# The last feed-forward output blocks computed by token halves, with the final norm of one half between the matmuls of the other

## The reference, cut to what matters

```python
def rmsnorm(x, g):
    y = x * lax.rsqrt(jnp.mean(x * x, axis=-1, keepdims=True) + EPS)
    return y * g
...
for l in range(DEPTH):                       # DEPTH = 1
    ...                                      # attention, gated DeltaNet, merge: x += gt1 * (...)
    h = rmsnorm(x, norm2_g[l]) * (1.0 + sc2) + sh2
    gate, up = jnp.split(h @ w_ffn_in[l], 2, axis=-1)
    x = x + gt2 * ((jax.nn.silu(gate) * up) @ w_ffn_out[l])
return rmsnorm(x, final_g)
```

## Time and profile before

| what | value |
|---|---|
| time, median of 3 runs | 1871.59 us (1869.07 to 1871.85) |
| the profiled execution, own time | 1867.37 us |
| its span in the trace | 1865.7 us |
| PE busy | 1775.3 us, 95% |
| DVE busy | 892.4 us, 48% |
| ACT busy | 473.4 us, 25% |
| mean granted clock of TensorE | 0.972 |

### The profile page before, as it was taken

The page is one execution under the profiler, slowest core; times in us unless marked ns, Lnnn a source line. Parts: engine busy times, 40 slices in busy tenths (PEclk is TensorE's granted clock), DMA queues, the critical chain, the costliest instruction groups (busy, mean ns, idle before and its releaser), DMA issues.

```text
span 1865.7 us, 22580 instructions
## 1 busy us (share of the span) xinstructions
PE 1775.3 (95%) x8387; PEld 1424.8 (76%) x8387; DVE 892.4 (48%) x1231; ACT 473.4 (25%) x861; POOL 164.4 (9%) x208
## 2 busy tenths in 40 slices
PE   5998879999999999999899979999999999999997
PEld 5876768888767777677678868888888888888876
DVE  6675566667534444444554344243333324333336
ACT  3334422222243333343321222111111111111101
POOL 1125551111001001010000000000000000000000
PEclk7899999999999999999999979999999999999998
DMA  7745555666423231340445110222022012102002
GB/s 246 213 117 171 173 167 181 180 183 187 130 76 108 74 82 65 91 129 34 163 165 192 54 53 26 65 68 57 12 67 66 29 40 67 56 11 67 23 0 102
DMA packets 208877, 186.13 MB, mean 100 GB/s; under 512 B 15481, under 2 KB 186618, under 8 KB 208826
## 3 DMA queue, kind: packets, MB, share of 16 engines
q1 hardware_dynamic: 201770, 160.01, 29.2%
q0 software_dynamic: 7056, 25.43, 3.5%
HBM read 140.58 MB, written 44.83 MB: 99 GB/s over the span
## 4 chain that ended last, share of the span: by engine, by line
PE 78%; DVE 4%; issue 2%; DMA 1%; ACT 1%; SPq 0%; DVEq 0%; ACTq 0%; POOLq 0%
PE pm L895 35%; PE ps L895 17%; PE pm L1220 12%; PE aT L1089 3%; PE aS L1112 3%; PE aT L1100 1%; PE gps L1034 1%; DVE asc L1765 1%; DVE a_raw L1763 1%; ACT w_hi L1267 1%; DMA yst<-yb_d 1%; PE pm L1184 1%; PE gps L1039 0%; DVE tmp L1886 0%; DVE xT L1947 0%
## 5 line engine op out<-in xcount | busy, mean ns | idle before, releaser
L1547 DVE TENSOR_TENSOR w_lo<-w_raw,w_hi 128x1024 fp32r<-128x1024 f32 x105 | 131.2, 1250 | 536.8 <-ACT w_hi L1267 525.7
L895 PE MATMUL pm<-act_hi,w_hi 128*128 128x512 f32 x832 | 257.4, 391 | 4.0 <-DVE act_lo L1596 4.0
L895 PE MATMUL pm<-act_lo,w_hi 128*128 128x512 f32 x832 | 257.3, 391 | 0.0
L895 PE MATMUL pm<-act_hi,w_lo 128*128 128x512 f32 x832 | 256.6, 390 | 0.0
L895 PE MATMUL ps<-act_hi,w_hi 128*128 128x512 f32 x720 | 253.7, 434 | 0.7 <-DVE est L1649 0.7
L1267 ACT ACTIVATE w_hi<-w_raw 128x1024 fp32r<-128x1024 f32 x105 | 110.7, 1055 | 503.4 <-PE pm L895 492.4
L895 PE MATMUL ps<-act_lo,w_hi 128*128 128x512 f32 x720 | 228.0, 398 | 0.0
L895 PE MATMUL ps<-act_hi,w_lo 128*128 128x512 f32 x720 | 226.2, 396 | 0.0
L895 PEld LDWEIGHTS pm<-act_hi,w_hi 128*128 128x128 f32 x832 | 156.5, 188 | 36.8 <-issue 4.2
L895 PEld LDWEIGHTS pm<-act_lo,w_hi 128*128 128x128 f32 x832 | 156.7, 188 | 33.0
L895 PEld LDWEIGHTS pm<-act_hi,w_lo 128*128 128x128 f32 x832 | 156.5, 188 | 33.1
(11 more groups left out here) (277 smaller groups left out, 2108.4 us busy)
## 6 DMA issues: line engine op xcount, KB each, us to landing
w_raw<-in_w_in_dram SPq DMA_DIRECT2D x45, 512.0 KB, 5.4
w_raw<-in_w_ffn_in_dram SPq DMA_DIRECT2D x44, 512.0 KB, 3.8
a_raw<-in_w_ada_dram SPq DMA_DIRECT2D x32, 512.0 KB, 4.1
f_raw<-in_w_ffn_out_dram SPq DMA_DIRECT2D x22, 512.0 KB, 4.3
adab<-in_w_ada_dram SPq DMA_DIRECT2D x8, 1024.0 KB, 7.8
pk_d<-pk SPq DMA_DIRECT2D x8, 768.0 KB, 3.9
qkva_d<-est POOLq DMA_DIRECT2D x12, 512.0 KB, 4.4
ast<-qkva_d SPq DMA_DIRECT2D x24, 256.0 KB, 6.2
```

What stands on the lines that cost most here:

```text
L895: ins = pe.matmul(dst[:, cols], wt[:, ds % 2, k, :], at[:, cols], start=(first and n == 0), stop=(last and n == 2))
L1547: dve.tensor_tensor(w_lo[:, ds % 2], w_raw[:, ds % NR], w_hi[:, ds % 2].bitcast(F32), ALU.subtract)\
```

## The change

The last pair's output pass is done in two rounds of 8 blocks of 512 tokens each (j = 0 to 15, half h = j // 8, block b = j % 8) instead of one round of 8 blocks of 1024. Each half block has 6 matmuls, one accumulation, one square and (for b = 1 to 6) one addition, all on 512 columns. PE puts the sums of the first half behind half block 10, and the transposes of the first four token groups behind half blocks 11, 12, 14 and 15. DVE puts the first half's rsqrt behind the accumulation of half block 11, and rows 0, 1 and 2 behind those of 12, 13 and 15. After half block 15 stand row 3, the fifth group of transposes, the sums and the rsqrt of the second half, and the other groups and rows. The transposes go into `pm[0]` and `pm[1]` by turns, so group t waits for row t - 2. The first four rows are written to `w_raw` (whose weights are no longer needed) instead of `frow`; `gbc` lies in `f_raw[:, 0]`, and is loaded when both halves of `o_lo` of the last pair are made (`olo_ready` 22) rather than behind an output block. Nothing is changed in what is computed.

```diff
--- before.py
+++ after.py
@@ -251,7 +251,6 @@
         with ExitStack() as st4:
             sbin(st4, "xT_kept", [P, KT, S])
             frow = sbin(st4, "frow", [P, NT, D])
-            gbc = sbin(st4, "gbc", [P, D])
 
         with ExitStack() as pst:
             ps = [psin(pst, f"ps{n}", [P, S]) for n in range(2)]
@@ -378,6 +377,15 @@
         def diagonal_d(dram_t, t, d):
             return dram_t[bass.ds(t, 1)].rearrange("a (h d) i j -> (a d) i h j", h=B_H)[d]
 
+        gbc = f_raw[:, 0, :]
+
+        def out_row(t):
+
+            return w_raw[:, t].rearrange("p k c -> p (k c)") if t < NR else frow[:, t, :]
+
+        def half(h):
+            return slice(h * HALF, (h + 1) * HALF)
+
         block = ctx.enter_context(nc.Block())
 
 
@@ -703,11 +711,11 @@
                 load_body(2, it)
                 load_body(3, it)
             load_body(10, 0)
-            sp.wait_ge(o_mm, 8 * 11 + LEAD)
-            sp.dma_start(gbc[:, :], bass.AP(final_g.tensor, 0, [[0, P], [1, D]])).then_inc(gbc_in, 16)
+            sp.wait_ge(olo_ready, 22)
+            sp.dma_start(gbc, bass.AP(final_g.tensor, 0, [[0, P], [1, D]])).then_inc(gbc_in, 16)
             for t in range(NT):
                 sp.wait_ge(row_ready, t + 1)
-                sp.dma_start(out[t * P:(t + 1) * P, :], frow[:, t, :]).then_inc(out_stored, 16)
+                sp.dma_start(out[t * P:(t + 1) * P, :], out_row(t)).then_inc(out_stored, 16)
             sp.wait_ge(out_stored, 16 * NT)
 
 
@@ -1240,19 +1248,55 @@
                 ffn_body(2, it)
                 ffn_body(3, it)
             ffn_body(10, 0)
-            ffn_out(10, 0, range(8))
-
-            token_sums(1)
-            for t in range(NT):
-                if t >= 4:
-                    pe.wait_ge(row_ready, t - 3)
+
+            pe.wait_ge(hlo_ready, 22)
+            pe.wait_ge(olo_ready, 22)
+
+            def last_out(j):
+
+                h, b = divmod(j, 8)
+                pe.wait_ge(po_free, 8 * 10 + j + 1)
+                dst = pm[2 + b % 2][:, half(h)]
+                for e in range(2):
+                    for n, (wt, at) in enumerate(((o_hi, h_hi), (o_hi, h_lo), (o_lo, h_hi))):
+                        ins = pe.matmul(dst, wt[:, e, b * P:(b + 1) * P], at[:, 0, e, half(h)],
+                                        start=(e == 0 and n == 0), stop=(e == 1 and n == 2))
+                ins.then_inc(o_mm, 1)
+
+            def last_sums(h):
+
+                pe.wait_ge(sqs_ready, 6 + 6 * h + 6)
+                for n, src in enumerate((tmp[:, half(h)], est[:, 1, half(h)])):
+                    if n:
+                        pe.wait_ge(sq_ready, 8 + 8 * h + 8)
+                    for t in range(4):
+                        col = n * 4 + t
+                        ins = pe.matmul(pm[2][:, h * HALF + col:h * HALF + col + 1], src[:, t * P:(t + 1) * P], ones[:, 0:1],
+                                        start=True, stop=True)
+                ins.then_inc(ss2_mm, 1)
+
+            def last_turn(t):
+
                 if t == 0:
                     pe.wait_ge(po_free, 8 * 11 + 2)
-                if t == 3:
-                    pe.wait_ge(ss_read, 2)
+                if t == 4:
+                    pe.wait_ge(po_free, 8 * 12 + 2)
+                if t >= 2:
+                    pe.wait_ge(row_ready, t - 1)
                 for k in range(KT):
-                    ins = pe.transpose(pm[(t + 1) % 4][:, k * P:(k + 1) * P], xT[:, k, t * P:(t + 1) * P], ident[:, :])
+                    ins = pe.transpose(pm[t % 2][:, k * P:(k + 1) * P], xT[:, k, t * P:(t + 1) * P], ident[:, :])
                 ins.then_inc(ft_mm, 1)
+
+            for j in range(16):
+                last_out(j)
+                if j == 10:
+                    last_sums(0)
+                if j in (11, 12, 14, 15):
+                    last_turn({11: 0, 12: 1, 14: 2, 15: 3}[j])
+            last_turn(4)
+            last_sums(1)
+            for t in range(5, NT):
+                last_turn(t)
 
 
         @block.scalar
@@ -1531,9 +1575,13 @@
                 ffn_body(3, it)
             ffn_body(10, 0, ahead=False)
             split_o(10, 0)
-            for b in range(8):
-                act.wait_ge(po_free, 8 * 10 + b + 3)
-                squares(1, b)
+            for j in range(16):
+                h, b = divmod(j, 8)
+                act.wait_ge(po_free, 8 * 10 + j + 3)
+                if b >= 3:
+                    act.wait_ge(sqs_ready, 6 + 6 * h + b - 2)
+                act.activation(tmp[:, half(h)] if b == 0 else est[:, b % 2, half(h)], xT[:, b, half(h)], ACT.Square)\
+                    .then_inc(sq_ready, 1)
 
 
         @block.vector
@@ -1967,16 +2015,53 @@
             ch = Chain(dve, vec_chain, base)
             ffn_body(10, 0, ahead=False)
             split_o(10, 0)
-            for b in range(8):
-                add_squares(1, b - 1)
-                accumulate(10, 0, [b])
-            token_rsqrt(1)
-
-            dve.wait_ge(gbc_in, 16)
-            for t in range(NT):
+
+            def last_add(j):
+
+                h, b = divmod(j, 8)
+                if 1 <= b <= 6:
+                    dve.wait_ge(sq_ready, 8 + j + 1)
+                    if b > 1:
+                        dve.wait_ge(sqs_ready, 6 + 6 * h + b - 1)
+                    dve.tensor_tensor(tmp[:, half(h)], tmp[:, half(h)], est[:, b % 2, half(h)], ALU.add)\
+                        .then_inc(sqs_ready, 1)
+
+            def last_x(j):
+
+                h, b = divmod(j, 8)
+                dve.wait_ge(o_mm, 8 * 10 + j + 1 + LEAD)
+                dve.scalar_tensor_tensor(xT[:, b, half(h)], pm[2 + b % 2][:, half(h)], gt2h[:, b:b + 1],
+                                         xT[:, b, half(h)], ALU.mult, ALU.add).then_inc(po_free, 1)
+
+            def last_rsqrt(h):
+
+                two = slice(4 * h, 4 * h + 4)
+                sums = pm[2][:, h * HALF:h * HALF + 8]
+                dve.wait_ge(ss2_mm, 1 + h + 1)
+                ch.link(dve.tensor_copy(rt[:, two], sums[:, 4:8]))
+                dve.tensor_tensor(ss[:, two], sums[:, 0:4], rt[:, two], ALU.add).then_inc(ss_read, 1)
+                dve.wait_ge(ss_read, 1 + h + 1)
+                ch.link(dve.tensor_scalar(ss[:, two], ss[:, two], 1.0 / D, EPS, ALU.mult, ALU.add))
+                rsqrt(ch, dve, ss[:, two], rr[:, two], rt[:, two])
+
+            def last_row(t):
+
+                dve.wait_ge(gbc_in, 16)
                 dve.wait_ge(ft_mm, t + 1)
-                dve.scalar_tensor_tensor(frow[:, t, :], pm[(t + 1) % 4][:, :], rr[:, t:t + 1], gbc[:, :],
+                dve.scalar_tensor_tensor(out_row(t), pm[t % 2][:, :], rr[:, t:t + 1], gbc,
                                          ALU.mult, ALU.mult).then_inc(row_ready, 1)
+
+            for j in range(16):
+                last_add(j - 1) if j else None
+                last_x(j)
+                if j == 11:
+                    last_rsqrt(0)
+                if j in (12, 13, 15):
+                    last_row({12: 0, 13: 1, 15: 2}[j])
+            last_row(3)
+            last_rsqrt(1)
+            for t in range(4, NT):
+                last_row(t)
 
 
 # ---- launch: one core; inputs and outputs as the reference has them ----
```

## The result

| | before | after |
|---|---|---|
| median of 20 runs each | 1869.89 us (1868.10 to 1872.81) | 1873.10 us (1870.14 to 1876.96) |
| ratio to before, 95% interval | | 1.0014 (1.0008 to 1.0021) |
| span of the profiled execution | 1865.7 us | 1871.1 us |
| from PE's first matmul of the last pair to the end of the span | 50.78 us | 53.75 us |

The changed kernel is slower by 0.14%, 2.6 us (1.5 to 3.9), less than the 0.2% that one would take for a difference in a short measurement, but with this many runs clear of no change. (The two medians lie 3.2 us apart, inside that interval.) The forecast was +1.6 us.

What follows compares the result with a forecast made beforehand. The prediction took a DVE-led chain of 51 us, the accumulate-square-add circle and the tail, as the bound. Steps summed to +2.2 us at the last row, less 0.6 at the stores: +1.6, median 1873.2 us, range 1868.5 to 1877.

Steps and rivals of the forecast that it cites:

- 1: accumulation 1 starts: Start of the last pair: after 12 matmuls, at 1819.60 us, the second half block's accumulation starts, instead of 1822.29.
- 2: a round; accumulation 7 starts: First half's half blocks: six rounds of 2.04 us, so accumulation 7 starts at 1831.84 us; PE waits in them.
- step 3: After accumulation 7 PE sets the pace: half blocks 9 and 10, first sums 1.95 us; accumulation 11 starts at 1838.9 us.
- step 4: From accumulation 11 DVE has no pause: 13.1 us of work to row 2's end; row 3 ends at 1853.3 us.
- step 5: PE's fifth transposes wait for row 2, second sums behind them: 3.7 us taken, between 2.65 (full clock) and 4.75 (half).
- 6: rsqrt: Second half's rsqrt, after the sums are done at 1855.85 us: ends at 1858.7 us.
- step 7: Rows 4 to 7 with two PSUM buffers: 5.45 us at half clock, 4.9 at full; last row ends at 1864.15 us.
- 8: from the last row's end to the end: Final stores: with four gone early, the last lands 2.8 us after issue instead of 3.4, giving back 0.6 us.
- a circle that halves do not shorten enough: DVE accumulates, ACT squares, DVE adds, then the next block: 3.545 us a round; two halves cost 4.08 us.
- The clock falls inside the half blocks: Rival: PE's pauses between half blocks bring half clock, deciding in the second half; about +8.5 us, 1880; chance 0.15.
- The halves are cheap: Rival: each half-block operation costs just half, round 1.77 us, PE keeps its clock; -3.1 us, 1868.5; chance 0.07.
- The interleaving does not hold: Rival: PE, stopped at transposes 2 until row 0 is read, delays half block 15; +4.6 us, 1876; chance 0.05.

Runs made afterwards that it cites:

- experiment 3: Changed kernel with nothing between its half blocks, sums, rsqrt, transposes and rows following half block 15 as in the kernel before: end 52.97 us, ratio 1.0004 to the kernel before.
- experiments 4: Kernel before with DVE accumulating block b before adding the square of block b - 1: end 48.13 us, ratio 0.9981 to the kernel before.
- 8: Changed kernel with DVE accumulating half block j before adding square j - 1: end 49.05 us, ratio 0.9988 to the kernel before.
- experiment 5: Changed kernel with accumulation before addition, second sums before the fifth transposes, and four PSUM buffers for the last four groups: end 44.93 us, ratio 0.9968 to the kernel before.
- 6: Kernel before with accumulation ahead of the addition, plus 12 unneeded matmuls on PE in front of the sums: end 46.24 us, ratio 0.9969 to the kernel before.
- the second experiment: Changed kernel with the second half's sums put in front of the fifth group of transposes on PE: end 47.45 us, ratio 0.9992 to the kernel before.

## Why the prediction was right, and by how much its terms were off

| step | forecast | measured |
|---|---|---|
| 1: accumulation 1 starts | 4.7 | 4.61 |
| 2: a round; accumulation 7 starts | 2.04; 16.9 | 2.05; 16.94 |
| 3: accumulation 11 starts | 24.0 | 23.97 |
| 4: row 3 ends | 38.4 | 38.1 |
| 5: from row 2's end to the sums done | 3.7 (2.65 to 4.75) | 4.45 to 4.6 |
| 6: rsqrt | 2.85 | 2.78 |
| 7: rows 4 to 7 | 5.45 | 6.40 |
| 8: from the last row's end to the end | 3.15 | 3.08 |
| end | 52.4 | 53.75 |

The mechanism held at each step: a circle that halves do not shorten enough, DVE's work in the second half, a new wait behind row 2, a rsqrt paid twice, two buffers where four had been. The 1.4 us by which the end is late lie in steps 5 and 7, less the 0.3 by which step 4 was overpriced, and both are about work at half clock. In step 5 I took a value between full and half clock, and most of it ran at half (0.59 on average). In step 7 the clock was foreseen and the term was mis-sized: I priced eight transposes at half clock at 1.3 us, and they take 1.7. The price came from a stretch of 1.2 us with 8 records in its row. But the count of a stretch has every record that touches it, those that reach in from outside too. The time from start to start, which the timeline has, is the measure: in the kernel after 16 transposes take 3.69 us on the chain, with the last one's latency, and group 7 lets its row start 1.71 us after group 6 does (1866.74 against 1865.03), so one takes some 0.21 us. At full clock it is 0.10 (group 0 to the next half block, 0.79 us for eight).

Two hits are in part luck. The measured median, 1873.10, lies 0.1 us from the 1873.2 that was forecast, but I had started from the median of three runs, 1871.6, and twenty gave 1869.89; the step itself, forecast at 1.6 us, was 2.6. And in step 3 two errors cancel: the 12 matmuls behind accumulation 7 take 3.03 us on the chain, not 2.72, and the first sums 1.68, not 1.95.

The Trainium skill's table (VectorE: DVE Perf Modes, the section on the TRN2 errata) would have made the halves' round some 1.9 us. The runs show 2.05, 747 ns for the accumulation and 690 for the addition. What it says of a fixed cost per instruction the trace agrees with in direction: cutting the instructions in two cost 0.55 us a block (2 x 2.05 against 3.545), and in the profile of experiment 3 2.2 us of it reach the end.

The rivals. *The clock falls inside the half blocks*: it does not, 1.00 from 1821.60 to 1835 with PE busy for 11.35 of 13.4 us by the records, and 1.00 in the rows of the second half up to 1852. The Trainium skill's case of short idles between matmul groups (TensorE: Matmul & The Clock Gate, the section on PSUM-queue depth-cycling) does not appear at these pauses. What the clock did cost, it cost after the pause behind the last half block. *The halves are cheap*: 747, 690 and 632 ns refute it. *The interleaving does not hold*: transposes 2 start at 1847.68, 0.24 us behind half block 14's last matmul and after row 0 (ended at 1847.29), so PE lost no time to that wait, as worked out.

The comparison that I had not made is the one with a better kernel before. I took the circle of 3.545 us as given and asked what halves do to it; experiments 4 and 8 show that the order of two DVE instructions made it, in both kernels.

What stays open: whether experiment 5 or 6 is the better one; what halves with the swapped order and nothing between them would do, which would show what the interleaving is worth by itself; and what decides in which executions the clock is low in the first blocks.

## What to carry to other kernels

Where an engine waits for another's result in each round and has independent work at hand, look first at the order of its own instructions: accumulating block b before adding the square of b - 1 took the circle away (3.5 us by the ratio, for one line), which splitting the blocks did not. When work of one half is put between the other's, put what the serial tail waits for first (here the sums) and what waits for a late row last; each instruction behind a waiting one inherits its wait. And short TensorE work behind a pause may run at half clock, as it did here after 3.2 us without work: price it from a row at that clock, and leave room for either.

## What the runs showed of the hardware that I had not expected

Useless matmuls made the profiled execution shorter, twice: in the pauses ahead of the sums they kept the granted clock at 1.00, and group 4 with the sums took 2.78 instead of 4.45 us, the sums of the unchanged layout 3.7 instead of 5.68.

The same pause of 3.69 us ahead of the last pair does not always bring the clock down: in the second experiment's execution the first 12 matmuls took 3.00 us at a granted clock of 1.00, in that of the kernel after 4.59, and in all others of this case with that pause 4.4 to 4.6.

At half clock eight transposes cost 1.7 us against 0.79 at full.

A store of 512 KB landed 2.6 us after its issue when stores were spaced, against a median of 3.1 in a train of eight; this is the kernel after's answer for the output's tile (minimum, median, maximum):

```profile
DMA to landing us min/median/max: 2.6/2.6/2.7
```
